# A stream of expert rows in which the rows of V are no longer taken in turns of four with those of U

## What is computed

```python
s_top, i_top = top_k(s, 16)                  # both halves of 8 heads, 128 keys each
best, sel = top_k(all pair sums, 16)         # 16 of 16384 experts a head
gate = softmax(best)                         # 8 * 16 = 128 weights a token
act = gelu(sum over d of x[d] * expert_u[e, d])   # for the 128 chosen e
y = sum over e of gate[e] * act[e] * expert_v[e]  # rows of 1024
```

## Time and profile before

| | |
|---|---|
| median of 3 runs | 3911.48 us (3911.21 to 3912.47) |
| the profiled execution: time | 3909.31 us |
| the profiled execution: span, first to last instruction | 3907.5 us |
| PE, DVE, ACT, POOL busy | 2361, 2365, 746, 2421 us |
| gathers | 2176 rows, 1141 MB, 76.9% of 16 DMA engines' span |
| first gather | at 479 us |

### The profile page before, as it was taken

How to read it: one execution, slowest core, us unless ns; L and a number is a source line. 1 busy time by engine, 2 the same in 40 slices (tenths; PEclk the granted TensorE clock), 3 DMA queues, 4 the chain that set the end, 5 groups by cost and what they waited for, 6 DMA issues and landing times. The chain is left out here.

```text
span 3907.5 us, 39453 instructions
## 1 busy us (share of the span) xinstructions
PE 2361.2 (60%) x13072; PEld 1485.0 (38%) x13072; DVE 2365.4 (61%) x6021; ACT 746.3 (19%) x1971; POOL 2421.0 (62%) x2180
## 2 busy tenths in 40 slices
PE   7877955676657845767578932665757850023354
PEld 6664745553424514545345602542424520000011
DVE  3464498967661379978661388977662369854400
ACT  3322124222021032222111031222021030000000
POOL 0000046877775667876675567877776667777776
PEclk9887977887878977878779966886878975556688
DMA  4101377999999999998899998998999999999999
GB/s 156 43 4 54 104 290 276 406 391 339 337 376 368 409 372 357 341 322 314 320 336 355 409 362 315 382 382 320 358 379 395 409 359 325 377 400 408 408 409 374
DMA packets 356414, 1273.68 MB, mean 326 GB/s; under 512 B 44698, under 2 KB 51930, under 8 KB 351476
## 3 DMA queue, kind: packets, MB, share of 16 engines
q0 software_dynamic: 313344, 1140.99, 76.9%
q1 hardware_dynamic: 42868, 130.17, 8.9%
HBM read 1265.91 MB, written 4.31 MB: 325 GB/s over the span
## 5 line engine op out<-in xcount | busy, mean ns | idle before, releaser
L2994 POOL DMA_INDIRECT slots<-in_peer_expert_u,table x1013 | 1204.3, 1189 | 907.5 <-DVE table L2311 478.6
L2406 DVE SCALAR_TENSOR_TENSOR slots<-slots,xe 128x1024 f32<-128x1024 f32 x992 | 1186.5, 1221 | 390.4 <-DMA slots<-in_peer_expert_u,table 360.7
L2994 POOL DMA_INDIRECT slots<-in_peer_expert_v,table x1004 | 1036.2, 1032 | 459.2 <-issue 280.4
L1462 PE MATMUL ps<-slots,band 128*32 128x512 f32 x4016 | 719.0, 790 | 725.1 <-DMA slots<-in_peer_expert_v,table 644.9
L1462 PEld LDWEIGHTS ps<-slots,band 128*32 128x32 f32 x4016 | 154.6, 130 | 1108.4 <-issue 1069.4
L846 PE MATMUL ps<-region_h,region_w 128*128 128x288 f32 (+1 forms) x1024 | 265.1, 420 | 77.5 <-ACTq L2527 61.4
L882 PE MATMUL ps<-arena,region_h 128*128 128x256 f32 (+5 forms) x1120 | 249.4, 380 | 19.7 <-ACT region_t L2558 16.0
L846 PEld LDWEIGHTS ps<-region_h,region_w 128*128 128x128 f32 x1024 | 206.8, 205 | 134.0 <-issue 73.7
L1402 PE MATMUL ps<-region_h,region_w 128*128 128x288 f32 (+1 forms) x1024 | 255.9, 404 | 0.0
L1402 PEld LDWEIGHTS ps<-region_h,region_w 128*128 128x128 f32 x1024 | 192.8, 193 | 81.5 <-issue 44.8
L2191 DVE MAX8 region_c<-ps 128x8 f32<-128x128 f32 x136 | 33.6, 289 | 310.6 <-PE ps L1387 203.6
(11 more groups left out here) (466 smaller groups left out, 3702.7 us busy)
## 6 DMA issues: line engine op xcount, KB each, us to landing
region_w<-in_w_in SPq DMA_DIRECT2D x64, 512.0 KB, 6.8
region_w<-in_peer_w_query SPq DMA_DIRECT2D x64, 512.0 KB, 7.3
arena<-in_w_in SPq DMA_DIRECT2D x20, 1024.0 KB, 8.6
slots<-in_peer_expert_u,table POOLq DMA_INDIRECT x1013, 6.6
slots<-in_peer_expert_v,table POOLq DMA_INDIRECT x1004, 7.8
arena<-in_w_out SPq DMA_DIRECT2D x12, 1024.0 KB, 10.0
region_h<-in_w_out SPq DMA_DIRECT2D x4, 1024.0 KB, 7.8
region_v<-in_peer_sub_keys SPq DMA_DIRECT2D x8, 512.0 KB, 24.6
```

The source lines that it names most:

```text
L1462: mm = nc.tensor.matmul(ps[32 * j:32 * j + 32, 6 + half_, :], window(m % BAND, row), row_at((1, m), k.g)[:, half_ * 512:(half_ + 1) * 512] ...
L2406: V.scalar_tensor_tensor(rows, rows, 1.0, xe[:, u, :], ALU.mult, ALU.mult, accum_out=own).then_inc(x_.u_free, 1)
L2994: G.indirect_dma_start(row_at(what, k.g), None, rows, bass.IndirectOffsetOnAxis(ap=numbers, axis=0)).then_inc(loaded[slot], 16)
```

## The change

In the loop that lays out a stage, a V row that is wanted was held back at every multiple of four until four U rows had gone out since, as long as U rows were left. That condition is taken away.

```diff
             wanted = u < len(self.spread) and now >= self.spread[u] + 2 * LAG - LAND
             k = rows[j][1]
-            if wanted and (i == len(rows) or k % 4 or all(kind == 0 for _, kind, _, _ in self.fetches[-4:])):
+            if wanted:
                 self.fetches.append((now, 1, u, k))
                 j += 1
```

## The result

| | before | after |
|---|---|---|
| median of 4 runs | 3911.35 us | 3971.61 us |
| lowest to highest | 3898.62 to 3912.47 | 3955.45 to 3975.31 |
| profiled execution, its span | 3909.31, 3907.5 us | 3955.45, 3953.6 us |
| ratio of the runs, 95% interval | | 1.0156 [1.0127, 1.0185] |

The change makes the kernel 60 us slower by the medians. The profiled execution of after is the lowest of its four runs, so the two traces show 46 us of it; the other 14 can't be placed in them.

The account below looks back on a forecast made before the run. It took the kernel as a stream of 2176 row gathers with DMA nearly always busy. Terms 7 + 16 + 12 + 46 - 18 = +63 on the profiled 3909.3, 2.2 under the median, gave about 3974; 8-in-10 range 3912 to 4018.

Parts of the forecast that it names:

- a: Last stage, no layer beside it: separate V and U rows cost 275 us against 268, +7, bounds 3 and 12.
- b: Hand-over from stage 1 to 2: 24 more V rows remain, 30 us later with 14 back, +16, bounds 0 and 37.
- c: Hand-overs 0 to 1 and 2 to 3: V2 waits for U2's chain, about +6 each, +12, bounds 0 and 15 each.
- d: U runs beside the layer: DVE at 92% busy makes them longer, +26, 0, +22, rounded to +46, bounds +14 and +80.
- e: V runs beside the layer: dots leave DVE, stretches shrink by 3% of 613 us, -18, bounds -66 and +14.
- the sign that another wait holds the layer: In the U runs: DVE's share staying under 85% while the span grows would show the forecast wrong.
- At 92%: U runs beside the layer: with DVE 92% busy the three stretches take 218, 177 and 212 us.
- the other sign: V runs beside the layer: coming out 10% shorter or more would show the forecast wrong.
- The wait on ACT's order: U runs: ACT standing in order before the gelu of tile 1 until its last dot, if DVE stays under 85%.
- Faster, by the V run: Rival: V runs beside the layer shrink by more than 81 of 613 us, result 3866 to 3870; chance 0.09.
- Nothing: Rival: DMA is the bound throughout, slow U runs and quick V runs cancel, about 3911, within 0.2%; chance 0.05.
- The hand-overs dominate: Rival: empty stretches idle DMA, no layer work gives them back, +116, about 4027; chance 0.14.

Follow-up runs that it names:

- the change again: The unaltered changed kernel run once more beside the other runs, against the kernel before: 3958.76 us, ratio 1.0144.
- stage 1 whole: The change made in stage 1 alone, against the kernel before: 3911.86 us, ratio 1.0022.
- waits filled: V runs in stages 0 to 2 with last V rows kept for the wait behind the next tile's U, last stage in turns, against before: 3922.04 us, ratio 1.0069.
- the kernel with runs and filled waits: V runs, last 24 or 28 rows kept for the wait, against before: 3931.22 us; the +20 is its version with the last stage in turns, 3922.04 us.
- unfilled waits alone: Turns of four kept, but rows that filled the waits moved ahead of them, against the kernel before: 3967.25 us, ratio 1.0165.

## Why the prediction came out right, and where its parts did not

Forecast 3974, measured 3971.61; slower, as forecast. The sum is nearer than its terms. Since the profiled execution shows 46 us of the 60, the terms are held against those 46 and the runs' ratios.

| term | forecast | trace of after | by runs |
|---|---|---|---|
| a, last stage | +7 | +5 from V0's first gather on (+11 in the change again) | +12 (4 to 21) |
| b, hand-over 1 to 2 | +30, with 14 back in the layer | +30, layer 2 -19 | stage 1 whole: +9 (1 to 16) |
| c, hand-overs 0 to 1, 2 to 3 | +6, +6 | +16, +5 | not alone |
| d, U runs | +26, 0, +22 | +23, +11, +26 | d and e of all three, waits filled: +27 |
| e, V runs | -18 | -50 | as above |

**a** was right in size and in make-up: V at 1.26, U at 1.36. Its PE is idle there as forecast. The forecast DVE share near 90% is 108.69/120 = 91%, and at the turn to V1 POOL never waits for PE longer than 0.7 us, with less than 3 forecast.

**b** was right in place and mechanism: "a DVE wait for stage 2's first U row of some 40 us in place of 13" is 40.87, 40.73 and 40.62 in the three kernels that have the change in stage 1. The term's hand-over is +30 and its return 19 to 20 where 14 was put.

**c** was right at one hand-over and mis-sized at the other. The step "by then 13 slots are filled, so POOL ends V2 about 15 us later. Net about 6 each" failed at the first: the hand-over is +16, just past its bound of 15, for V2's first sum stood 34.39 us and a wait of 14.21 on DVE came behind it. At the second, the last of the route's scores on PE and DVE's first dot of stage 3, before:

```profile
L1387 PE MATMUL ps<-arena,region_c x256: 272/275/553, 448.9 to 3154.9; 128*128 128x128 f32 x128
...
3215.05 1.21 DVE L2406 SCALAR_TENSOR_TENSOR slots<-slots,xe 128x1024 f32<-128x1024 f32 x1
```

This dot comes 60.2 us behind the scores. In after the scores end at 3191.7 and the dot is the one at 3257.20 above, 65.5 behind: +5, as forecast, and the change again gives +5 too. Together 22 against 12.

**d** came to 60 where 46 was taken, and its reason holds only in part. It took DVE as the bound at 92% busy; DVE was busy 192.41/215 = 89%, 152.25/194 = 78% and 179.65/216 = 83%. Two of these are under the 85% that I had named as the sign that another wait holds the layer, and there the step "At 92%" fails; the V runs, 8% shorter, stayed under the 10% that would have been the other sign. Stage 1, for which I put 0, lost 11. What the prediction left out is POOL: gathers of 1.38 us with 0.3 between them and, in stage 0, no wait. Its price for a gather beside dots was the last stage's, 1075 ns, which has no layer beside it.

That POOL is the cause of the loss isn't shown, though. DVE's waits for U rows (us, times, longest) in stage 0's stretch, 968:1160 before and 958:1173 in after, and in stage 2's, 2755:2945 and 2766:2982:

```profile
DVE slots L2406 <- DMA slots<-in_peer_expert_u,table: 21.6, 10, 6.0
...
DVE slots L2406 <- DMA slots<-in_peer_expert_u,table: 12.8, 21, 1.3
...
DVE slots L2406 <- DMA slots<-in_peer_expert_u,table: 40.4, 18, 5.3
...
DVE slots L2406 <- DMA slots<-in_peer_expert_u,table: 17.0, 16, 3.8
```

These waits fell, while DVE's busy time rose by 69 and 63 us. Had every row come in time, the two stretches could be at most some 14 us (with 1.6 for rows in the extra slots) and 17 us shorter, an estimate from these waits, of the 23 and 26 that they lost. So DVE's own work makes part of the loss, as forecast, and the slower stream at most the rest; halving the dots relieves both at once and can't part them. The wait on ACT's order that I named as the alternative would stand as a wait for slots on POOL, and in the U runs of stages 0 and 2 there is none over 1.5 us.

Here the Trainium skill's rule must be held against the runs again. SBUF — State Buffer, "Who interferes with whom", says that a DVE instruction with two SBUF inputs contends with a GpSimd instruction that reads SBUF, and infers, for another instruction of that kind, that descriptor generation is not held by it. The runs do not bear that out: halving these DVE instructions alone took the gathers beside them from 1.37 to 1.01 us. That a port is what slows them isn't shown either. And it is not the full block of the same section: whole dots at 96% of DVE's time stood beside gathers of 0.99 us in one execution (below).

**e** is the term furthest off: -50 where -18 was taken, inside its bounds of -66 and +14. The step that failed is the pace it was taken by, "that is 3% of 613": the V runs came out 8% shorter. The count beside it, "busy 171, 189 and 160 us", was too high as well. PE was busy 150, 167 and 142. In stage 0's stretch the sums took 40.95 us for 60 rows before and 64.30 for 120 in after, 0.68 and 0.54 us a row, since the clock was higher: the granted clock of these stretches is 0.91, 0.87 and 0.89, against 0.79, 0.79 and 0.76 in the earlier trace rows, with the two levels being 2.4 and 1.2 GHz. V rows on end keep PE busy with sums and layer, and it gets more of its higher level. In the U runs it has less, 0.66, 0.70 and 0.61 against 0.77, 0.78 and 0.75. PE's share in them is 79, 85 and 81%, over the forecast 80 in two of three and under the 90 that would have spoken for the faster rival.

**The sum** was made of terms as if they stood in a row. They do not: the layers of after, -11, lie 31 below those of the kernel with runs and filled waits (+20). My reading of that is that the stretch without fetches relieves the layer that runs through it and bills it at the hand-over. In the prediction's own bookkeeping the layers were to lose 46 - 18 - 14 = 14, the hand-overs 30 + 12 = 42 and the last stage 7; the trace has -11, 47 + 5 = 52 and 4, and 1 ahead of the first layer. So it was right that the hand-overs carry the larger part, two thirds in the forecast. That the total came within 3 us is luck: the layers were 25 us too dear and the hand-overs 10 too cheap, and some 14 us that the trace doesn't hold made up for most of what was left.

**The rivals.** *Faster, by the V run* needed the V runs to shrink by 81 of 613 us: they shrank by 50. (The shares given for and against it were a little high: over the three stretches of the earlier trace rows DVE was 73% busy, not 75, and PE 67%, not 70.) *Nothing* is out, by 60 us: the DMA slices are nearly as full as before, at 324 GB/s in stage 0's U run and 387 in its V run, so full slices didn't hold the time. *The hand-overs dominate* was right about where the loss lies (unfilled waits alone cost 1.65%) and wrong on its size, since b's hand-over came to 30 of the 37 and with a return in the layer, c to 22 of 30, and e to -50 in place of -18; its 60 for d is what was measured.

## What to carry to other kernels

Where an in-order stream feeds two consumers, first look at what fills the stream while one consumer's chain has yet to finish: rows moved out of that wait cost as much here as the whole reordering, and the bill came at the next stage's start, where nothing had been edited. Mixing the kinds paid by itself too (0.7%); turns shorter than the consumer's batch of four lost 1.3%. Price an issue instruction by a row from beside the work that it will run beside, not from a quiet stage.

## What the runs showed of the hardware that was not expected

**The gather's length beside dots differs from execution to execution.** In the last stage the kernel after and the one with the change there alone have equal code, and their U rows alone go at 120/88 = 1.36 and 130/85 = 1.53 us. The quickest such stretch is that of the kernel with runs and filled waits. Windows, and POOL's group in them, of that kernel and then of the one changed in the last stage alone:

```profile
3610.00:3725.00 115.00, 1.55 (x8) 0.00 (x0) 110.85 (x181) 0.00 (x0) 87.61 (x89) 0.51 1.03 409
...
L2994 POOL DMA_INDIRECT slots<-in_peer_expert_u,table x82 | 80.9, 986 | 25.3 <-issue 24.7 <-PE ps L1462 0.6
```
```profile
3610.00:3740.00 130.00, 0.00 (x0) 0.00 (x0) 105.71 (x175) 0.00 (x0) 104.40 (x85) 0.50 0.95 342
...
L2994 POOL DMA_INDIRECT slots<-in_peer_expert_u,table x79 | 99.6, 1261 | 24.1 <-issue 24.1
```

89 rows in 115 us at 409 GB/s, 88 in 120 in the kernel after, and 85 in 130 at 342. POOL waits for next to nothing in any of them, DVE is the busiest in the quickest one, and V rows alone move at 409 GB/s in before and after. What sets the gather between 0.99 and 1.26 us is open. Over the stage's 104 U rows it is worth 24 us (133 us for all of them in the quickest trace, 157 in the slowest), which is of the size by which runs of one kernel differ (3895 to 3935 us for the change in the last stage alone). Beside a layer it repeats: in stage 0's U run a gather takes 1.35 to 1.40 us in each of the five traces that have one with whole dots.

**A shorter dot goes with a shorter gather.** Halving the dots is worth 226 us, and POOL's gathers in a U run go from 1.37 to 1.01 us with it. How much of the 226 is POOL's and how much DVE's own was not measured.
